# A channel fold by reflection, gate groups in half steps, and a last tile in column groups

## The chip, the cores and the metric

The program runs on all 8 cores of one Trainium2 chip. Each core holds one sequence of the batch (4096 positions, 1024 channels), and the cores exchange nothing. A time is the device time in microseconds (us) of the slowest core. Engines are named as in the profile: PE (TensorE matmul), PEld (its weight loads), DVE (VectorE), ACT (ScalarE), POOL (GpSimd), SP (SyncE, which here only issues transfers). L412 is line 412 of the kernel.

## The reference

Two layers with plain residual adds, then a final RMSNorm. `rms_norm` divides by the root mean square over 1024 channels.

```python
def fourier_mixer(h, w_in, w_out):            # layer 0
    proj = h @ w_in                           # (S, 2E), E = 2048
    xin, z = proj[..., :E], proj[..., E:]
    xg = xin.reshape(b, s, 8, 256)            # 8 groups of 256 channels
    y = fft2(xg, axes=(1, 3), norm="ortho").real
    return (y * silu(z)) @ w_out
def sgu_mixer(h, ...):                        # layer 1, chunks of 128 positions
    proj = h @ w_in                           # (S, 3E)
    u, v = gelu(proj[..., :2 * E]) split in two
    z = proj[..., 2 * E:]
    v = layer_norm(v) ; v = w_s[g] @ v (per chunk, per group) + b_s
    return (u * v * silu(z)) @ w_out
for i in range(2):
    x = x + mixer[i](rms_norm(x, norm[i]), ...)
return rms_norm(x, final_norm)
```

## The kernel before

Five instruction streams are recorded by hand in one program order. A small class `Q` per engine adds the semaphore waits that the buffers of an instruction ask for; each engine then runs its own instructions strictly in the order in which they were recorded. Six PSUM banks `pf0` to `pf5` are handed out in turn by `next_f()`, whatever the use, so the seventh user of a bank since the first waits until the first was read out. Two more banks, `pb`, serve the transposes.

Layer 0 runs in these stages.

- Stage A, 32 steps `s`, one tile of 128 positions each. SP loads the tile `xt`, ACT squares and sums it (`square`, L391), POOL adds eps and takes the power -0.5 (`norm`, L399 and L401), DVE scales to bf16 `xn` (L403), PE transposes it (L495), DVE writes it into `hT` times the norm weight `g0T` (L500). PE also multiplies the tile by `tr`, the first factor of the position transform (L475), ACT and DVE copy the result to `U` (L269, L271), and SP stores it to `Ud` in DRAM. In between PE works off gate groups from the list `zq`: `zgroup(hb, zt)`, L412, is 8 matmuls of 512 positions into one bank, closed by one SiLU on ACT (L416) into `sz`. The order of the six first loads and three small constants (`ident`, `tr`, `gT`) is written out ahead of the loop, all on SP. Up to step 23 the factor matmuls run one step late (the list `due`); from step 24 they run in their own step.
- Block transform, `qd` from 7 down to 0. SP reads `Ud` back in another layout as `V`. For each `qd` and each of 8 channel blocks `dc`, PE does 4 matmuls of 128 columns against the table `bdt` (L571) into one bank; ACT or DVE, whichever has the smaller planned load (`ev_engine`), scales it into `H` (L558, L560). A whole gate group stands behind `dc` 3. For `qd` 0 a small matmul per `dc` (L579) gives four further columns.
- Fold, once per channel group `g` (`fold`, L431). The channel DFT is folded into the input projection: 256 rows of the branch weight, cast to bf16 by a POOL transfer (`load_wb`, buffers `wb`), are multiplied by a 256x256 table `fmat` of cosines and sines, two matmuls of 256 columns for each `dc`. ACT copies the four banks to `wp`, then one column to `wsp` (L438) and zeros over it (L440).
- Per group: `pq(g)`, L608, multiplies `wp` with `H`; ACT and DVE split the result into `Dt` and `St`; DVE multiplies them onto the gates in `sz` (`gate`, L639), and SP stores to `gy`. Then `fold(g + 1)` and the gate groups of later `zt` (`zall`). `tick()` spreads the casts of later weights (`precasts`, POOL transfers `w0d` and `wind`) and the stores over these steps. `last_column()` (L676) uses `wsp` in group 6.

Layer 1 runs eight rounds of four tiles (L764, L839, L866, L876). Its last tile is `last_tile`: two halves of 512 columns are added (L776) and squared (L778), POOL forms the factor (L780, L782), DVE applies factor and norm weight in one instruction per half (L786), and SP and ACT store one half each. The program ends with a barrier on all queues.

## Time and profile before

| what | value |
|---|---|
| median of 3 runs (lowest, highest) | 1567.16 us (1565.13, 1567.92) |
| profiled execution, its own time | 1564.49 us |
| span of its slowest core | 1563.1 us (cores 1561.1 to 1563.1) |
| PE busy | 1533.1 us, 98% |
| DVE, ACT, POOL busy | 48%, 33%, 10% |
| granted TensorE clock, mean | 0.998 |
| share of PE in the chain that ended last | 97% |
| stage A ends, first block matmul | 115.54 us |
| `pq(0)` starts | 149.73 us |
| first layer-1 matmul (L839) | 447.26 us |
| last matmul of the program issued | 1553.72 us |

The span runs from the first to the last instruction on a core; the execution's own time is 1.4 us longer. Busy times of PE are of modelled ends of pipelined matmuls, so a stretch is better read from the start of one row to the start of the next: `8 matmuls of a gate group` start 1.73 us apart from the next group. A row that says `[1.77 <-DVE U_70 L271]` was idle for 1.77 us before it, and what ended that was the DVE instruction of line 271 that wrote `U`.

### The profile page before, as it was taken

To read this page: it belongs to the slowest core of one execution; us is meant where nothing else is said; L and a number is where in the kernel's file an instruction comes from. 1 tells how busy PE (TensorE), PEld (TensorE's weight loads), DVE (VectorE), ACT (ScalarE), POOL (GpSimd) and SP (SyncE) were. 2 spreads that over 40 slices of the span, in tenths; PEclk is the share of its full clock that TensorE was granted. 3 is DMA by queue.
4 is the path that set the end of the run, shared out by engine and by line. 5 is a ranking of instruction groups with operands and counts; after the bars stand their busy time and mean duration, and the time that the engine had idled before them with its cause. 6 is when DMAs were issued, how large, how long until landed. Compare 5 with 4: busy or idle time off the path is not lost.

```text
span 1563.1 us, 25441 instructions; the slowest of 8 cores (1561.1 to 1563.1 us)
## 1 busy us (share of the span) xinstructions
PE 1533.1 (98%) x8458; PEld 779.5 (50%) x8458; DVE 744.1 (48%) x1241; ACT 517.5 (33%) x919; POOL 156.7 (10%) x336
## 2 busy tenths in 40 slices
PE   6999999999999999999999999999999999999997
PEld 3546766546744444544444454444444444544443
DVE  5767532212657335624543463356346435624552
ACT  6756333333233213322331332133123313322331
POOL 3311111110211011001001100110010011001000
PEclk9999999999999999999999999999999999999999
DMA  9976999999879933632464165345325632643411
GB/s 247 299 246 176 174 137 148 152 145 149 253 249 263 255 110 103 205 142 78 162 193 137 28 219 175 106 138 193 135 55 189 203 101 73 199 167 88 147 49 55
DMA packets 103299, 247.74 MB, mean 158 GB/s; under 512 B 40042, under 2 KB 56042, under 8 KB 87402
## 3 DMA queue, kind: packets, MB, share of 16 engines
q1 hardware_dynamic: 53652, 207.76, 41.5%
q0 software_dynamic: 15568, 29.63, 15.0%
q10 hardware_dynamic: 33952, 8.72, 2.9%
q8 instruction: 72, 1.18, 0.3%
q14 instruction: 55, 0.45, 0.1%
HBM read 225.24 MB, written 58.87 MB: 182 GB/s over the span
## 4 chain that ended last, share of the span: by engine, by line
PE 97%; DMA 1%; DVE 1%; issue 0%; ACT 0%; SPq 0%; POOL 0%; ACTq 0%; DVEq 0%; POOLq 0%
PE pf L764 28%; PE pf L866 28%; PE pf L839 14%; PE pf L412 14%; PE pf L608 7%; PE pf L876 2%; PE pf L431 1%; DMA a0x_55<-xt 1%; PE pf L571 1%; PE pb L495 1%; PE pf L475 1%; DMA gTs<-gT 0%; DVE hT L500 0%; SPq L166 0%; PE pf L676 0%
## 5 line engine op out<-in xcount | busy, mean ns | idle before, releaser
L764 PE MATMUL pf<-W_2523,u 128*128 128x512 bf16 x1024 | 222.3, 379 | 0.0
L764 PE MATMUL pf<-W_2512,gyt 128*128 128x512 bf16 x992 | 216.6, 379 | 0.0
L764 PEld LDWEIGHTS pf<-W_2523,u 128*128 128x128 bf16 x1024 | 100.2, 98 | 120.8
L764 PEld LDWEIGHTS pf<-W_2512,gyt 128*128 128x128 bf16 x992 | 97.1, 98 | 116.8
L869 ACT ACTIVATE u<-pf 128x512 bf16<-128x512 f32 x128 | 76.4, 597 | 164.0 <-PE pf L866 154.8
L843 ACT ACTIVATE v<-pf 128x512 f32<-128x512 f32 x128 | 75.2, 597 | 119.5 <-PE pf L839 102.2
L866 PE MATMUL pf<-h1T,ring_2519 128*128 128x512 bf16 x416 | 95.3, 379 | 0.0
L866 PE MATMUL pf<-h1T,ring_2518 128*128 128x512 bf16 x416 | 95.0, 379 | 0.0
L866 PE MATMUL pf<-h1T,ring_2522 128*128 128x512 bf16 x416 | 94.8, 379 | 0.0
L866 PE MATMUL pf<-h1T,ring_2520 128*128 128x512 bf16 x416 | 94.8, 379 | 0.0
L866 PE MATMUL pf<-h1T,ring_2521 128*128 128x512 bf16 x384 | 88.3, 379 | 0.0
L618 DVE TENSOR_TENSOR Dt_93<-pc_97,pf 128x256 bf16<-128x256 f32 x28 | 11.8, 421 | 144.4 <-PE pf L608 144.4
L880 DVE SCALAR_TENSOR_TENSOR ytmp_2531<-pf,gTs,TT 128x512 f32<-128x512 f32 x64 | 48.1, 751 | 47.9 <-PE pf L876 47.9
L755 POOL TENSOR_SCALAR sm_2545<-sm_2545 128x1 f32<-128x1 f32 x24 | 5.3, 221 | 617.5 <-ACT sqj L800 573.9
L866 PEld LDWEIGHTS pf<-h1T,ring_2518 128*128 128x128 bf16 x416 | 39.7, 98 | 43.4
L866 PEld LDWEIGHTS pf<-h1T,ring_2522 128*128 128x128 bf16 x416 | 39.7, 98 | 43.2
L866 PEld LDWEIGHTS pf<-h1T,ring_2520 128*128 128x128 bf16 x416 | 39.6, 98 | 43.2
L866 PEld LDWEIGHTS pf<-h1T,ring_2519 128*128 128x128 bf16 x416 | 39.6, 98 | 42.7
L869 ACT ACTIVATE sg_2542<-pf 128x512 bf16<-128x512 f32 x64 | 38.2, 597 | 68.1 <-PE pf L866 53.3
L869 ACT ACTIVATE sg_2543<-pf 128x512 bf16<-128x512 f32 x64 | 38.2, 597 | 65.4 <-PE pf L866 64.8
L608 PE MATMUL pf<-H,wp_84 128*128 128x260 bf16 x512 | 57.6, 274 | 0.0
L608 PE MATMUL pf<-H,wp_85 128*128 128x260 bf16 x512 | 57.4, 274 | 0.0
(298 smaller groups left out, 2308.8 us busy)
## 6 DMA issues: line engine op xcount, KB each, us to landing
ring_2519<-wind SPq DMA_DIRECT2D x20, 1024.0 KB, 8.2
ring_2520<-wind SPq DMA_DIRECT2D x19, 1024.0 KB, 7.7
ring_2521<-wind SPq DMA_DIRECT2D x19, 1024.0 KB, 7.2
ring_2522<-wind SPq DMA_DIRECT2D x19, 1024.0 KB, 7.8
ring_2518<-wind SPq DMA_DIRECT2D x19, 1024.0 KB, 7.8
gyt<-gy SPq DMA_DIRECT2D x7, 2048.0 KB, 16.2
wind<-w_in1p POOLq DMA_DIRECT2D x24, 512.0 KB, 46.7
V<-ud SPq DMA_DIRECT2D x32, 256.0 KB, 8.0
```

The costliest lines, as they stand in the source:

```text
L412: pe.op(lambda e: e.matmul(bank[:], w[:, dc, :], hT[:, dc, hb * 512:(hb + 1) * 512], start=(dc == 0), stop=(dc == 7)), [wb_, hTb[hb], hTal ...
L431: pe.op(lambda e: e.matmul(bank[:, h * 256:(h + 1) * 256], wb[wb_slot(2 * g + kc)][0][:, dc * 128:(dc + 1) * 128], fmat[:, kc, :], start=( ...
L475: pe.op(lambda e: e.matmul(bank[:], tr[:], xn_[:, h * 512:(h + 1) * 512], start=True, stop=True), [trb, xnb], [bb], waw=False)
L495: pe.op(lambda e: e.transpose(out=bank[:, dc * 128:(dc + 1) * 128], in_=xn_[:, dc * 128:(dc + 1) * 128], identity=ident[:]), [xnb, identb] ...
L608: pe.op(lambda e: e.matmul(bank[:, 0:HQ], w_[:, dc, cs * 128:(cs + 1) * 128], H[:, qd, dc, cs, :], start=(dc == 0), stop=(dc == 7)), [wpb, ...
L764: pe.op(lambda e: e.matmul(bank[:], lhs(kc), rhs[:, kc, nh * 512:(nh + 1) * 512], start=(kc == 0), stop=(kc == 15)), lb(kc) + rb(kc), [bb] ...
L839: pe.op(lambda e: e.matmul(bank[:], h1T[:, dc, t * 128:(t + 1) * 128], r_[:, dc, :], start=(dc == 0), stop=(dc == 7)), [h1Tb[t], rb], [bb] ...
L843: act.op(lambda e: e.activation(out=vj, in_=bank[:], func=AF.Gelu_apprx_tanh), [bb], [vjb])
L866: pe.op(lambda e: e.matmul(bank[:], r_[:, dc, c0:c0 + 128], h1T[:, dc, :], start=(dc == 0), stop=(dc == 7)), h1Tb + [rb], [bb], waw=False, ...
L869: act.op(lambda e: e.activation(out=out_ap, in_=bank[:], func=func), [bb], wb_)
L876: pe.op(lambda e: e.matmul(bank[:, t * 128:(t + 1) * 128], vhat[t][0][:, ct * 128:(ct + 1) * 128], wsT[:, ct // 2, :], start=True, stop=True),
L880: dve.op(lambda e: e.scalar_tensor_tensor(out=y_[:].rearrange("c (t p) -> c t p", p=128), in0=bank[:].rearrange("c (t p) -> c t p", p=128) ...
```

## The change

Five things are done together. The diff below is cut to its core; of `last_tile` it shows the added lines alone.

1. The fold uses the symmetry of the DFT. Row `c` and row `256 - c` of the branch weight (the rows 0 and 128 as a pair of their own) are loaded as f32 in pieces `st` (128 rows x 2 x 256) by SP, and POOL writes their sum and difference as bf16 into `eo`. The table falls to 128 rows: 129 cosine columns for the sums (`fE`) and 192 columns for the differences (`fO`, 64 of them shared with the first). Of the sixteen 256-column matmuls of a group, eight have 129 columns and eight 192. Channels within a group are reordered (`_HARM`) to fit, on the host, for the weights too. The casts through POOL's transfers (`load_wb`) go. 8 groups have 4 pieces each, 64 POOL instructions in all: pieces 0 to 3 in stage A, 4 to 11 in the block transform, the rest by `tick()`. The casts of later weights start at tick 10 and then come every third tick instead of every fourth.
2. A gate group may be cut in two halves of 4 matmuls (`zhalves`). In the block transform the first half stands behind `dc` 3 and the second behind `dc` 7, with the bank taken at the first. The small matmuls of `qd` 0 go into one bank, ahead of it, and are read out by two DVE instructions.
3. `fold(1)` moves from behind `pq(0)` to the end of the block transform.
4. Stage A: the three small constants go to ACT's queue; the factor matmuls run one step late up to step 30; the norms run two tiles ahead up to step 14 and three from 15 on (before: three from 10 on).
5. The last tile has column groups of 512, 256 and 256, each with its own 16 matmuls; DVE applies the norm weight per group ahead of the factor, and the factor is then applied by ACT to one half and by DVE to the other.

```diff
+            def eo_of(g):
+                return eo[g if g < 3 else 4 - g % 2]
+            def load_piece(n):
+                t_, b_ = st[n % 2 if 4 <= n < 12 else 0]
+                sp.dma(t_[:], wb_in[n // 4, n % 4], d_st[n % 2 if 4 <= n < 12 else 0], writes=[b_], waw=True)
+            def sum_piece(n):
+                t_, b_ = st[n % 2 if 4 <= n < 12 else 0]
+                eo_, eob = eo_of(n // 4)
+                q = n % 4
+                for k, op in enumerate((ALU.add, ALU.subtract)):
+                    pool.op(lambda e: e.tensor_tensor(out=eo_[:, k, q * 256:(q + 1) * 256], in0=t_[:, 0, :],
+                                                      in1=t_[:, 1, :], op=op), [b_], [eob], waw=False)
+            folded = {"n": 0, "summed": 12}
+            def sums():
+                for n in range(12, 32):
+                    while n >= 20 and folded["n"] < n // 4 - 1:
+                        yield
+                    load_piece(n)
+                    for _ in range(4):
+                        yield
+                    sum_piece(n)
+                    folded["summed"] += 1
+                    yield
+                    yield
 
...
+                for _ in zhalves(hb, zt):
+                    pass
+            def zhalves(hb, zt):
 
                 w, wb_ = wz[zt % 6]
                 o, ob = sz[zt % 6]
                 bank, bb = next_f()
                 for dc in range(8):
+                    if dc == 4:
+                        yield
...
+                while folded["summed"] < 4 * g + 4:
+                    next(summing)
                 for d2 in dcs:
                     bank, bb = next_f()
                     for h in range(2):
                         dc = 2 * d2 + h
-                        for kc in range(2):
-                            pe.op(lambda e: e.matmul(bank[:, h * 256:(h + 1) * 256],
-                                                     wb[wb_slot(2 * g + kc)][0][:, dc * 128:(dc + 1) * 128], fmat[:, kc, :],
-                                                     start=(kc == 0), stop=(kc == 1)),
-                                  [wb[wb_slot(2 * g + kc)][1], cpkb], [bb], waw=False, inc=(h == 1 and kc == 1))
+                        for k, f, a, z in ((0, fE, 0, 129), (1, fO, 64, 256)):
+                            pe.op(lambda e: e.matmul(bank[:, h * 256 + a:h * 256 + z], eo_[:, k, dc * 128:(dc + 1) * 128], f,
+                                                     start=(k == 0), stop=True, skip_group_check=(k == 1)),
+                                  [eob, cpkb], [bb], waw=False, inc=(h == 1 and k == 1))
...
+            act.dma(ident[:], c_id[:, :], d_const, writes=[identb])
+            act.dma(gT[:], gT_in[:, :], d_cg, writes=[cG])
+            act.dma(tr[:], c_tr[:, :], d_tr[0], writes=[trb])
+            for t in range(NX):
+                load_x(t)
...
-            then = {0: [1], 1: [], 2: [], 3: [4], 4: [6], **{s: [s + 2] for s in range(5, 10)}, 10: [12, 13]}
+            then = {0: [1], 1: [], 2: [], 3: [4], 4: [6], **{s: [s + 2] for s in range(5, 15)}, 15: [17, 18]}
...
-                due.append(s)
-                while len(due) > (s < 24):
-                    transform(due.pop(0))
+                if s > 0:
+                    transform(s - 1)
                 for _ in range((s != 4) + (s % 4 == 3 and s < 16)):
                     if zq:
                         zgroup(*zq.pop(0))
+                if s == 31:
+                    transform(s)
...
-                if s in (12, 14):
-                    load_wb(s // 2 - 6)
+                if s in (12, 16, 20, 24):
+                    sum_piece(s // 4 - 3)
+                if s in (8, 12, 16, 20):
+                    load_piece(s // 4 - 2)
+                if s in (28, 29):
+                    load_piece(s - 24)
...
-                if ticks["n"] % 4 == 1:
+                if ticks["n"] > 8 and ticks["n"] % 3 == 1:
                     next(casts, None)
+                next(summing, None)
...
+                halves = zhalves(*zq.pop(0))
...
-                    if qd > 0 and dc == 3:
-                        zgroup(*zq.pop(0))
...
+                    if dc % 4 == 3:
+                        next(halves, None)
                 if 0 < qd < 5:
                     fold(0, [4 - qd])
+                for n in ((4,), (5, 6), (7,), (8,), (9,), (10,), (11,), ())[7 - qd]:
+                    sum_piece(n)
+                    if n < 10:
+                        load_piece(n + 2)
                 if qd == 0:
-                    load_wb(2)
-                    load_wb(3)
-                    for i in range(6, 9):
+                    fold(1, range(4))
+                    for i in (6, 7, 10):
                         load_wz(i)
-                    load_wb(4)
-                    load_wb(5)
-                    for i in range(9, 11):
-                        load_wz(i)
-                    for _ in range(2):
-                        next(casts, None)
-            zgroup(*zq.pop(0))
...
+            def last_tile(n):
 
                 x_, xb = x1[n % NX1]
+                y_, yb = x1[(n + 1) % NX1]
                 sm_, smb = sm[n % 4]
+                cols = [slice(0, 512), slice(512, 768), slice(768, 1024)]
+                xh = [Buf(f"xh{h}") for h in range(3)]
+                yh = [Buf(f"yh{h}") for h in range(3)]
+                for h, c in enumerate(cols):
+                    bank, bb = next_f()
+                    w = c.stop - c.start
+                    for kc in range(16):
+                        pe.op(lambda e: e.matmul(bank[:, 0:w], u[:, kc, 384:512], W1[:, kc, c],
+                                                 start=(kc == 0), stop=(kc == 15)),
+                              [ub[kc], W1b[kc // 4]], [bb], waw=False, inc=(kc == 15))
+                    dve.op(lambda e: e.tensor_tensor(out=x_[:, c], in0=x_[:, c], in1=bank[:, 0:w], op=ALU.add),
                            [bb, xb], [xh[h]])
                     act.op(lambda e: e.activation(out=sqj[:, c], in_=x_[:, c], func=AF.Square, scale=1.0 / 32.0,
                                                   accum_out=sm_[:, h:h + 1]), [xh[h]], [sqjb, smb], waw=False)
+                    if h == 1:
+                        pool.op(lambda e: e.tensor_scalar(out=sm_[:, 0:1], in0=sm_[:, 0:1], scalar1=EPS, scalar2=sm_[:, 1:2],
+                                                          op0=ALU.add, op1=ALU.add), [smb], [smb], waw=False)
+                    dve.op(lambda e: e.tensor_tensor(out=y_[:, c], in0=x_[:, c], in1=gFt[:, c], op=ALU.mult),
+                           [xh[h], gFb], [yb, yh[h]], waw=False)
+                pool.op(lambda e: e.tensor_tensor(out=sm_[:, 0:1], in0=sm_[:, 0:1], in1=sm_[:, 2:3], op=ALU.add), [smb], [smb])
                 pool.op(lambda e: e.tensor_tensor(out=sm_[:, 0:1], in0=sm_[:, 0:1], in1=mhalf[:], op=ALU.pow),
                         [smb, mhalfb], [smb])
+                for h, c in ((0, cols[0]), (1, slice(512, 1024))):
+                    if h == 0:
+                        act.op(lambda e: e.activation(out=y_[:, c], in_=y_[:, c], func=AF.Copy, scale=sm_[:, 0:1]),
+                               [yh[0], smb], [yh[0]])
+                    else:
+                        dve.op(lambda e: e.tensor_scalar(out=y_[:, c], in0=y_[:, c], scalar1=sm_[:, 0:1], scalar2=None,
+                                                         op0=ALU.mult), [yh[1], yh[2], smb], [yh[1]])
+                    (act, sp)[h].dma(out[n * 128:(n + 1) * 128, c], y_[:, c], d_last[h], reads=[yh[h]], writes=[outb])
```

How the instructions stand, at three places. First PE at the start of the block transform (`V` is its input, `wz` a gate group's weights, `pf` the bank written), before, the rest of `qd` 7 and the head of `qd` 6:

```order
L571 MATMUL pf3<-bdt_92,V_52 128x128 x4
L412 MATMUL pf4<-hT_51,wz3_81 128x512 x8
L571 MATMUL pf5<-bdt_92,V_52 128x128 x4
L571 MATMUL pf0<-bdt_92,V_52 128x128 x4
L571 MATMUL pf1<-bdt_92,V_52 128x128 x4
L571 MATMUL pf2<-bdt_92,V_52 128x128 x4
L571 MATMUL pf3<-bdt_92,V_52 128x128 x4
L571 MATMUL pf4<-bdt_92,V_52 128x128 x4
L571 MATMUL pf5<-bdt_92,V_52 128x128 x4
```

and after the change, the same place:

```order
L623 MATMUL pf3<-bdt_91,V_52 128x128 x4
L450 MATMUL pf4<-hT_51,wz3_81 128x512 x4
L623 MATMUL pf5<-bdt_91,V_52 128x128 x4
L623 MATMUL pf0<-bdt_91,V_52 128x128 x4
L623 MATMUL pf1<-bdt_91,V_52 128x128 x4
L623 MATMUL pf2<-bdt_91,V_52 128x128 x4
L450 MATMUL pf4<-hT_51,wz3_81 128x512 x4
L623 MATMUL pf3<-bdt_91,V_52 128x128 x4
L623 MATMUL pf4<-bdt_91,V_52 128x128 x4
```

The gate group in `pf4` stood whole between two blocks of the same `qd`; it now ends only behind the last block of its `qd`, and the second block of the next `qd` takes the same bank `pf4` again, one block after it.

Second POOL in stage A around step 12 (`stats` are the norm's sums, `wb` the cast weight, `eo` the sums of the fold), before:

```order
L399 TENSOR_SCALAR stats_47<-stats_47 128x1
L401 TENSOR_TENSOR stats_47<-stats_47,mhalf_49 128x1
L166 DMA wb0_86<-wbT 128x1024
L399 TENSOR_SCALAR stats_47<-stats_47 128x1
L401 TENSOR_TENSOR stats_47<-stats_47,mhalf_49 128x1
```

and after:

```order
L431 TENSOR_SCALAR stats_47<-stats_47 128x1
L433 TENSOR_TENSOR stats_47<-stats_47,mhalf_49 128x1
L397 TENSOR_TENSOR eo0_86<-st0_99 128x256 x2
L431 TENSOR_SCALAR stats_47<-stats_47 128x1
L433 TENSOR_TENSOR stats_47<-stats_47,mhalf_49 128x1
```

A transfer for the fold stood between the norms of two tiles; now two POOL computations stand there, and the next tile's norm behind them.

Third DVE at the end of the program (`x1` are the tiles, `gFt` the final norm weight, `sm` the factor), before:

```order
L894 SCALAR_TENSOR_TENSOR x1_4_2538<-x1_4_2538,sm1_2546,gFt_2537 128x1024
L894 SCALAR_TENSOR_TENSOR x1_0_2514<-x1_0_2514,sm2_2547,gFt_2537 128x1024
L776 TENSOR_TENSOR x1_1_2515<-x1_1_2515,pf4 128x512
L776 TENSOR_TENSOR x1_1_2515<-x1_1_2515,pf5 128x512
L786 SCALAR_TENSOR_TENSOR x1_1_2515<-x1_1_2515,sm3_2548,gFt_2537 128x512 x2
```

and after:

```order
L825 TENSOR_TENSOR x1_1_2569<-x1_1_2569,pf3 128x512
L832 TENSOR_TENSOR x1_2_2570<-x1_1_2569,gFt_2591 128x512
L825 TENSOR_TENSOR x1_1_2569<-x1_1_2569,pf4 128x256
L832 TENSOR_TENSOR x1_2_2570<-x1_1_2569,gFt_2591 128x256
L825 TENSOR_TENSOR x1_1_2569<-x1_1_2569,pf5 128x256
L832 TENSOR_TENSOR x1_2_2570<-x1_1_2569,gFt_2591 128x256
L842 TENSOR_SCALAR x1_2_2570<-x1_2_2570,sm3_2602 128x512
```

The norm weight stands in instructions of its own behind each add, and behind the factor only one instruction of 512 columns is left on DVE.

## Rows read from the trace of the kernel before

**Rows 1.** The page's engine part: busy us, share of the span, instructions.

```profile
PE 1533.1 (98%) x8458; PEld 779.5 (50%) x8458; DVE 744.1 (48%) x1241; ACT 517.5 (33%) x919; POOL 156.7 (10%) x336
```

**Rows 2.** The chain that ended last: start us, us, what; two stretches of folds.

```profile
270.58 1.75 PE pf L431 x16
...
385.33 3.51 PE pf L431 x32
```

**Rows 3.** Timeline of PE, block transform: start us, us, instruction, count, idle before.

```profile
115.54 1.06 PE L571 MATMUL pf<-bdt,V 128*128 128x128 bf16 x16
116.43 1.89 PE L412 MATMUL pf<-hT,wz_81 128*128 128x512 bf16 x8
118.16 1.78 PE L571 MATMUL pf<-bdt,V 128*128 128x128 bf16 x28
...
120.23 0.38 PE L571 MATMUL pf<-bdt,V 128*128 128x128 bf16 x4 [0.29 <-ACT H L558]
...
149.73 14.35 PE L608 MATMUL pf<-H,wp_84 128*128 128x260 bf16 x128
```

**Rows 4.** Timeline of ACT there: a gate group's SiLU, then read-outs of blocks.

```profile
118.42 0.60 ACT L416 ACTIVATE sz_75<-pf 128x512 bf16<-128x512 f32 x1 [0.86 <-PE pf L412]
...
119.40 2.42 ACT L558 ACTIVATE H<-pf,g0s 128x512 bf16<-128x512 f32 x4 [0.38 <-PE pf L571]
```

**Rows 5.** Waits of PE: who waited for whom, us in total, times, longest.

```profile
PE pf L676 <- ACT wsp L438: 0.3, 1, 0.3
```

**Rows 6.** Timeline of all engines at the start, first tiles of stage A.

```profile
8.48 1.01 PE L495 MATMUL pb<-ident,a0xn_60 128*128 128x128 bf16 x8 [8.48 <-DVE a0xn_60 L403]
...
10.65 1.23 DVE L500 TENSOR_TENSOR hT<-pb,gTs 128x1024 bf16<-128x1024 bf16 x1 [2.44 <-DMA gTs<-gT]
...
11.79 0.76 DVE L403 TENSOR_SCALAR a0xn_61<-a0x_55,stats 128x1024 bf16<-128x1024 f32 x1
12.15 0.83 POOL L401 TENSOR_TENSOR stats<-stats,mhalf 128x1 f32<-128x1 f32 x1
12.64 0.33 SPq L166 DMA_DIRECT2D a0x_55<-xt  x1
```

**Rows 7.** Busy us by engine, clock, DMA share and GB/s, in two stretches.

```profile
10.00:20.00 10.00, 5.99 (x37) 3.40 (x38) 7.46 (x8) 7.19 (x14) 6.66 (x12) 1.00 1.03 253
...
150.00:200.00 50.00, 50.00 (x374) 36.23 (x372) 25.42 (x80) 17.85 (x39) 12.40 (x21) 1.00 1.04 170
```

**Rows 8.** Timeline of PE at step 24 of stage A.

```profile
83.40 1.89 PE L412 MATMUL pf<-hT,wz_81 128*128 128x512 bf16 x8 [1.77 <-DVE U_70 L271]
```

**Rows 9.** Timeline of POOL in stage A, one norm and the next.

```profile
77.38 0.57 POOL L401 TENSOR_TENSOR stats<-stats,mhalf 128x1 f32<-128x1 f32 x1 [0.21 <-POOL stats L399]
79.60 0.22 POOL L399 TENSOR_SCALAR stats<-stats 128x1 f32<-128x1 f32 x1 [1.65 <-ACT a0xn_61 L391]
```

**Rows 10.** POOL by shape: count, busy us and mean ns, idle before.

```profile
L639 POOL TENSOR_TENSOR szsp<-p_100,szsp 8x1792 bf16<-8x1792 f32 x1 | 3.3, 3289 | 0.1
...
L639 POOL TENSOR_TENSOR szsp<-p_100,szsp 8x224 bf16<-8x224 f32 x1 | 0.6, 610 | 0.1
```

**Rows 11.** Timeline of all engines over the last tile.

```profile
1539.74 13.98 PE L764 MATMUL pf<-W_2523,u 128*128 128x512 bf16 x64
...
1547.88 1.06 ACT L800 ACTIVATE sqj<-x_0_2514 128x1024 bf16<-128x1024 f32 x1 [5.76 <-DVE x_0_2514 L797]
...
1553.83 0.69 DVE L776 TENSOR_TENSOR x_1_2515<-x_1_2515,pf 128x512 f32<-128x512 f32 x1 [1.36 <-PE pf L764]
1554.61 0.63 ACT L778 ACTIVATE sqj<-x_1_2515 128x512 bf16<-128x512 f32 x1 [1.33 <-DVE x_1_2515 L776]
...
1556.75 1.42 DVE L786 SCALAR_TENSOR_TENSOR x_1_2515<-x_1_2515,sm_2548,gFt 128x512 f32<-128x512 f32 x2 [2.24 <-POOL sm_2548 L782]
...
1558.25 0.38 ACTq L166 DMA_DIRECT2D out<-x_1_2515  x1
```

**Rows 12.** Timeline of DVE: an add of 256 columns from PSUM.

```profile
151.84 0.42 DVE L618 TENSOR_TENSOR Dt_93<-pc_97,pf 128x256 bf16<-128x256 f32 x1 [3.19 <-PE pf L608]
```

More of the change, by code:

```diff
@@ L19 @@
 HQ = 260
+_HARM = [*range(0, 128, 2), *range(1, 128, 2)]
 def _chan_order():
@@ L23, in _chan_order @@
     for g in range(8):
-        o += [g * 256 + m for m in range(128)]
-        o += [g * 256 + 128] + [g * 256 + 256 - m for m in range(1, 128)]
+        o += [g * 256 + m for m in _HARM]
+        o += [g * 256 + 128] + [g * 256 + 256 - m for m in _HARM[1:]]
     return np.array(o)
@@ L65, in rows @@
         return a.reshape(4, 32, -1).transpose(1, 0, 2).reshape(128, -1)
-    pk = np.concatenate([Fm.reshape(128, 512), rows(B64)], axis=1)
+    pk = np.concatenate([FE, np.zeros((128, 1)), FO, rows(B64)], axis=1)
     bdt = np.stack([rows(BD[pr]) for pr in range(32)], axis=1)
@@ L347, in build @@
             wp = [tile(f"wp{i}", [128, 8, 256], BF16) for i in range(2)]
-            wb = [tile(f"wb{i}", [128, D], BF16, (top["at"] - 4096 if i < 2 else vh + 2048 * (i - 2)) + 2048 * (i % 2 if i < 2 else 0))
-                  for i in range(6)]
+            eo = [tile(f"eo{i}", [128, 2, D], BF16, o) for i, o in enumerate((top["at"] - 4096, wzo, wzo + 4096, vh + 4096, vh))]
             bdt, bdtb = tile("bdt", [128, 32, 128], BF16, top["at"])
@@ L354, in build @@
             wsT, wsTb = tile("wsT", [128, 8, 128], BF16)
+            st = [tile("st0", [128, 2, 256], F32, top["at"] - 2048), tile("st1", [128, 2, 256], F32, top["at"] - 4160)]
             assert top["at"] <= nc.sbuf_usable_end, (top["at"], nc.sbuf_usable_end)
@@ L363, in build @@
             d_wz = [dsem(f"d_wz{i}") for i in range(6)]
-            d_wb = [dsem(f"d_wb{i}") for i in range(6)]
+            d_st = [dsem(f"d_st{i}") for i in range(2)]
             d_gy = [dsem(f"d_gy{i}") for i in range(6)]
@@ L515, in build @@
                     sp.dma(Ud[r, 0:128, :], U[r % 8][0][:], d_us[r % 8], reads=[U[r % 8][1]], writes=[Udb])
-                for n in then.get(s, [s + 3] if 10 < s < 29 else []):
+                for n in then.get(s, [s + 3] if 15 < s < 29 else []):
                     norm(n)
@@ L564, in build @@
             for qd in range(7, -1, -1):
+                halves = zhalves(*zq.pop(0))
+                if qd == 0:
+                    bank, bb = next_f()
+                    for dc in range(8):
+                        pe.op(lambda e: e.matmul(bank[:, dc * 64:(dc + 1) * 64], V[:, 0, dc * 128:(dc + 1) * 128], b64,
+                                                 start=(dc == 0), stop=(dc == 7)), [Vb[0], cpkb], [bb], waw=False, inc=(dc == 7))
+                    for c in range(2):
+                        dve.op(lambda e: e.tensor_tensor(
+                            out=H[:, :, :, c, 256:260].rearrange("d q e t -> d e q t"),
+                            in0=bank[:].rearrange("d (e c q t) -> d c e q t", c=2, q=8, t=4)[:, c],
+                            in1=g0s[:].rearrange("d (e q t) -> d e q t", q=1, t=1).broadcast_to([128, 8, 8, 4]),
+                            op=ALU.mult), [bb, g0sb], Hb, waw=False, cost=cd(256))
                 for dc in range(8):
@@ L903, in build @@
                 if g == 0:
-                    fold(1, range(4))
                     for hb in range(6, 8):
@@ L919, in build @@
                     fold(g + 1, range(4))
+                if g == 1:
+                    for i in (8, 9):
+                        load_wz(i)
                 for zt in zafter[g]:
```

78 lines of the change are left out of this document (25 added, 53 removed).

## The prediction

> **What bounds the kernel now.** I read the engine part of the page first, then the chain that ended last, then the waits of PE, and last the timelines of the stretches that the change touches. PE is busy for 98% of the span [rows 1], so only two things can move the time: columns that PE no longer streams, and stretches in which PE stands still. From the first `pq` at 149.73 us to its last matmul at 1553.7 us PE runs without a gap worth naming, and a matmul taken out there is worth its full length. The gaps lie in three places: stage A, the block transform, and the tail behind the last matmul. The change has an edit in each, beside the shorter fold.
>
> **The fold, groups 2 to 5.** A group is sixteen matmuls of 256 columns in 1.75 us [rows 2], 109.4 ns each. Sixteen of 128 columns take 116.43 - 115.54 = 0.89 us [rows 3], 55.6 ns each, so a column costs (109.4 - 55.6) / 128 = 0.42 ns. 129 columns are 56.0 ns and 192 are 82.5 ns; eight such pairs are 1.11 us in place of 1.75 us, 0.64 us less. Four groups stand between PE work that never waits: **-2.57 us**, between -2.3 and -2.7.
>
> **Groups 6 and 7** follow each other (3.51 us, [rows 2]) and would give 1.29 us. But PE already waits 0.3 us for the `wsp` of group 7 [rows 5], behind eight read-outs on ACT that do not get shorter. These begin when the first bank is full, after 0.28 us in place of 0.44 us. I take that 0.16 us, **-0.16 us**; the ends are 0 and -1.29 us.
>
> **The block transform, with groups 0 and 1.** Today the stretch takes 149.73 - 115.54 = 34.19 us [rows 3], and group 1 another 1.75 us behind `pq(0)`: 35.94 us. PE's own work in the new stretch, per `qd`: eight blocks of 0.222 us and one gate group of 118.16 - 116.43 = 1.73 us [rows 3] are 3.51 us. The half steps even out the read-outs, since a half group of 0.86 us now stands behind every four blocks. But the bank does not follow. It is taken at the first half, is full only after the second, and five banks are handed out in between or right behind. The order rows show it: `pf4` is ended by the second half, then comes one block in `pf3`, and the next block wants `pf4` again. It must wait for the SiLU. From the end of a gate group to the SiLU's start are 118.42 - 118.16 = 0.26 us [rows 3, 4], the SiLU takes 0.60 us [rows 4], and from the end of a read-out on ACT (119.40 + 2.42 / 4 = 120.01) to PE's next matmul at 120.23 are 0.22 us [rows 3, 4]: 1.08 us. One block covers 0.22 us of it, so PE stands for 0.86 us; where a part of the fold (0.28 us) stands there, 0.80 us. That gives 4.37 us for each of three `qd` without fold, 13.1 us; 3.51 + 0.28 + 0.80 = 4.59 us for each of four with it, 18.4 us; for `qd` 0 3.51 us and at most 0.44 us for its small matmuls; then group 1, 1.11 us, with the same wait of 0.80 us inside it. Sum 37.4 us, **+1.4 us**. If the wait were not there it would be 37.4 - 3 x 0.86 - 5 x 0.80 = 30.8 us, -5.1 us; if ACT were each time at the start of another read-out of 0.60 us, +6.2 us. I stay at the worked value, since in the 0.86 us of the second half ACT can finish what the four blocks left it.
>
> **Stage A.** Three terms. First, at step 24 two tiles' factor matmuls fall together and PE waits 1.77 us for a bank [rows 8]. With the steps late by one throughout, this goes; at step 31 a gate group now stands between the two: -1.8 us. Second, `hT` of the first tile waits 2.44 us for `gT`, which SP issued behind three tiles; DVE starts it at 10.65 us though PE's transposes ended at 8.48 + 1.01 = 9.5 us, so DVE, the next norm and with it the next load at 12.64 us are about 1.0 us late [rows 6]. On ACT's queue `gT` leaves ahead of the tiles. But the transfer engines are full in that stretch, share 1.03 [rows 7], so an earlier issue is only partly an earlier landing: I take half, -0.5 us, between 0 and -1.0. Third, POOL gets two sums of 256 elements for each of four pieces, between the norms of two tiles. The nearest rows are sums over 8 partitions: 3289 ns for 1792 elements, 610 ns for 224 [rows 10], 1.71 ns an element and 0.66 us for 256. Two with the gaps between them are 1.5 us, and POOL idles 1.65 us a step [rows 9]. They fit, just; for the piece that lands late I add 0.3 us. Upper end: 128 partitions could cost more than 8; at 2.0 us a sum the pair exceeds the idle by 2.5 us, four times: 10 us. Stage A: **-2.0 us**, between -2.8 and +8.
>
> One mechanism speaks against this. POOL's power instruction took 0.83 us at 12.15 us [rows 6] where it takes 0.57 us elsewhere [rows 9], and it ran while DVE's norm at 11.79 us occupied its 0.76 us: POOL was held up by 0.26 us. The Trainium skill, page "SBUF — State Buffer", section "Who interferes with whom", says that DVE and GpSimd share one pair of ports as an exclusive lock, so that a DVE instruction in a two-port mode or with two SBUF inputs and a GpSimd instruction block each other for a whole instruction. By that rule the trace agrees, and what it would do is the second rival below.
>
> **The tail.** PE ends at 1539.74 + 13.98 = 1553.72 us, and the last store is issued 4.53 us later, at 1558.25 us [rows 11]. The last add falls from 0.69 us to 0.42 us for 256 columns [rows 11, 12]. The square falls by (1.06 - 0.63) / 2 = 0.215 us [rows 11]. POOL keeps two instructions. In place of 1.42 us for two DVE instructions in a row one of 512 runs beside one on ACT, some 0.6 us (0.63 us for an ACT row of 512 with a sum). That is 0.27 + 0.215 + 0.8 = 1.3 us; the multiplications that now stand between the adds on DVE may cost 0.1 us: **-1.2 us**, between -0.5 and -1.6. PE's columns stay 1024.
>
> **At no cost.** The pieces from 12 on, the paced casts and the moved weight loads run while PE never waits, in a stretch where the transfer engines are full anyway (share 1.04, [rows 7]); each fold has its four pieces summed at least 9 ticks, 16 us, ahead. If that cover went, PE would wait for a landing at a fold.
>
> **Sum.** -2.57 - 0.16 + 1.4 - 2.0 - 1.2 = -4.5 us. The rows come from an execution of 1564.49 us (span 1563.1 us), which would become 1560.0 us. That execution lies 2.7 us under the median of the runs shown; taken off the median, 1567.16 us, the forecast is 1562.6 us.
>
> **Rivals.** *The half steps do as they look:* the bank wait is hidden and the block transform becomes PE's own work. For it: today's waits there are only 0.3 us each [rows 3]. Against it: the bank order above. -11.0 us, 1556.2 us.
>
> *No change that can be told:* stage A gives nothing. Tiles land no earlier in a full transfer stretch, and a norm on DVE in the way of a pair of sums, as in rows 6, lengthens the pair by 0.76 us to 2.3 us, 0.6 us over POOL's idle, four times, 2.4 us. For it: [rows 6, 7]. Against it: the 1.77 us of step 24 has nothing to do with either. Stage A then stands near 0, and the sum is -2.5 us, 1564.7 us.
>
> *Slower:* the sums on POOL hold up the norms, and PE waits for transposes at steps 12 to 24. SP waits with POOL, since the next piece needs the buffer `st0`, and the next tiles' loads stand behind it in SP's queue. Against it: the 0.66 us of rows 10, if partitions work side by side. It decides from about 1.75 us a sum (3.7 us a pair, 2.0 us over the idle, 8 us in all, which turns -4.8 us into +3.1 us); at 2.0 us a sum it is +5.4 us, 1572.6 us.
>
> **How the numbers follow.** Forecast 0.52, half steps as they look 0.10, no change 0.26, slower 0.12. A measurement of this kernel tells about 0.2% from no change, 3.1 us. The forecast's own range is 1559.5 to 1565.0 us, of which 0.85 lies beyond 3.1 us. Faster: 0.44 + 0.10 + a fifth of the no-change case, 0.05, about 0.6. Same: 0.08 + 0.19 + 0.03, 0.3. Slower: 0.1, nearly all from the slow case. The range, 1558.0 to 1567.5 us, leaves out most of the first rival and of the slow one.
>
> **What would show it.** Right: folds of 1.11 us where 1.75 us stood; PE waits of about 0.8 us on `sz` in each `qd` of the block transform, and about 37 us from the first block matmul to `pq(0)`; no wait at step 24; 3.2 us from the last matmul to the last store's issue. Wrong: no waits on `sz` there (first rival), first block matmul not earlier than 115 us (second), sums of over 1.5 us and PE waiting for norms after step 12 (third), or PE waiting on `eo` or on `sz` stores behind 150 us, for which I see no cause.

## The result and the profile after

The change made the kernel slower: 1585.22 us (median of 4 runs, 1583.14 to 1587.31) beside 1567.16 us of the kernel before on the same chip, a ratio of 1.0118 [1.0096, 1.0140] (in brackets the 95% interval), some 18 us. Medians and ratios, here and below, are of undisturbed executions; some others ran longer, at a lower granted clock on one die or both, and are left out. The forecast was 1562.6 us and faster. The cores of the traced execution, which lay within 2 us before, now spread from 1571.2 to 1585.0 us. All rows of after are of core 1, the slowest. The waits of PE between 150 and 420 us (who waited for whom, us in total, times, longest), where before there was only the `wsp` of [rows 5]:

```profile
PE pf L450 <- ACT sz_74 L454: 16.7, 1, 16.7
PE pf L472 <- POOL eo_89 L397: 4.9, 1, 4.9
PE pf L650 <- ACT wp_84 L480: 1.0, 1, 1.0
```

The first two are the two that the last paragraph of the prediction named as having no cause in sight. The chain that ended last, traced in this stretch (start us, us, what), shows what stands behind them:

```profile
183.03 1.14 PE pf L472 x16
185.93 1.79 POOL eo_89 L397 x2
187.79 10.54 DMA st_99<-wbE
...
331.40 0.72 POOL eo_90 L397
332.19 11.01 DMA st_99<-wbE
344.04 0.72 POOL eo_90 L397
344.83 11.33 DMA st_99<-wbE
356.34 0.65 issue
356.99 0.72 POOL eo_90 L397
358.31 15.57 DMA gy<-sz_74
373.96 0.61 ACT sz_74 L454
374.70 19.45 PE pf L450 x80
```

From 186 to 358 us the path is no longer PE but a ladder, and each of its rungs has two parts: a piece lands (10 to 17 us), POOL sums it, and only then can SP ask for the next one, since there is one tile `st0`. The same on SP's queue (start us, us from the first to the last of the run of issues, count):

```profile
199.95 43.72 SPq L172 DMA_DIRECT2D st_99<-wbE  x4
243.81 0.47 SPq L172 DMA_DIRECT2D gy<-sz_76  x1
244.43 0.57 SPq L172 DMA_DIRECT2D gy<-sz_77  x1
256.64 44.16 SPq L172 DMA_DIRECT2D st_99<-wbE  x4
...
316.61 41.50 SPq L172 DMA_DIRECT2D st_99<-wbE  x4
358.31 0.47 SPq L172 DMA_DIRECT2D gy<-sz_74  x1
```

A row of four issues is the time from the first to the fourth, so three rungs: they take 41 to 44 us, and a pair of stores stands between each four. (The expectations below call such a row "four pieces".) On POOL the casts stand behind the sums, so a late piece holds them back too, and each rung then lets out two casts at once (timeline of POOL, `wind` is a cast; "idle before" shows the wait for the piece):

```profile
241.86 1.40 POOL L397 TENSOR_TENSOR eo_90<-st_99 128x256 bf16<-128x256 f32 x2 [10.27 <-DMA st_99<-wbE]
243.22 1.39 POOL L172 DMA_DIRECT2D wind<-w_in1p  x2
255.15 1.42 POOL L397 TENSOR_TENSOR eo_90<-st_99 128x256 bf16<-128x256 f32 x2 [10.54 <-DMA st_99<-wbE]
```

The store of `sz_74` leaves at 358.31 us, lands at 374, and until then the SiLU that refills `sz_74` may not run: PE fills six banks and stands. After its stand it does not even start at full speed. The windows (length, busy us of PE, PEld, DVE, ACT and POOL with counts, granted clock, DMA share, GB/s):

```profile
349.00:358.00 9.00, 8.99 (x42) 3.88 (x40) 0.00 (x0) 0.00 (x0) 1.70 (x3) 1.00 1.01 115
358.00:374.70 16.70, 0.00 (x0) 0.03 (x1) 0.00 (x0) 0.74 (x2) 3.79 (x6) 0.61 0.99 200
374.70:380.20 5.50, 5.50 (x17) 2.04 (x18) 0.00 (x0) 2.90 (x6) 0.00 (x0) 0.62 0.99 166
380.20:394.00 13.80, 13.80 (x66) 6.24 (x65) 0.00 (x0) 4.78 (x8) 3.48 (x5) 1.00 0.71 122
```

In the 16.7 us without a matmul the granted clock was 0.61 in the mean; it was 1.00 at their start and 0.50 at their end, the lower of the two levels (1.2 of 2.4 GHz). The next 17 matmuls took 5.5 us where 42 took 9.0 us before the stand: about 1.9 us more. The 4.9 us for `eo` were lost earlier: the fold of group 5 starts at 316.78 us, at a granted clock of 0.52 from 316 to 321 us, and takes 2.10 us in place of 1.14. So 4.9 + 1.0 + 16.7 + 1.9 = 24.5 us are lost between 311 and 380 us on this core. The wait for `sz_74` is there on all eight cores (7.8 to 19.7 us), that for `eo` on two.

The other parts lost nothing of this. Block transform, timeline of PE:

```profile
114.31 1.05 PE L623 MATMUL pf<-bdt,V 128*128 128x128 bf16 x16
...
117.82 0.39 PE L623 MATMUL pf<-bdt,V 128*128 128x128 bf16 x4
118.82 0.83 PE L623 MATMUL pf<-bdt,V 128*128 128x128 bf16 x12 [0.61 <-ACT sz_75 L454]
...
151.00 1.16 PE L650 MATMUL pf<-H,wp_84 128*128 128x260 bf16 x9
```

It takes 36.7 us with group 1, against 35.94, the same on every core. It begins at 114.31 us; [rows 3] with 115.54 are of core 7, and on core 1 it began at 114.31 before, too. The bank wait on the SiLU is there in each `qd`, about 0.6 us long. The tail, timeline of all engines:

```profile
1569.50 7.11 PE L822 MATMUL pf<-W_2577,u 128*128 128x512 bf16 x48
...
1579.91 0.38 ACTq L172 DMA_DIRECT2D out<-x_2_2570  x1
```

1579.91 - 1576.61 = 3.30 us from the last matmul to the last store's issue, 4.53 us before [rows 11].

### The profile page after: what moved, and what is told of

It reads as the page before. It is cut to its first block, busy times and chain, and to the rows that moved or that the text cites. A ratio compares the mean times of both kernels' runs of the same rounds, so it can differ in the third digit from the quotient of the medians.

```text
span 1585.0 us, 25600 instructions; the slowest of 8 cores (1571.2 to 1585.0 us)
## 1 busy us (share of the span) xinstructions
PE 1535.2 (97%) x8474; PEld 780.1 (49%) x8474; DVE 749.6 (47%) x1241; ACT 519.4 (33%) x919; POOL 196.6 (12%) x385
## 4 chain that ended last, share of the span: by engine, by line
PE 83%; DMA 11%; issue 2%; POOL 1%; ACT 1%; DVE 1%; SPq 0%; POOLq 0%; DVEq 0%; ACTq 0%
PE pf L921 28%; PE pf L806 27%; PE pf L894 14%; DMA st_99<-wbE 9%; PE pf L450 5%; PE pf L650 4%; PE pf L931 2%; DMA gy<-sz_74 1%; PE pf L623 1%; PE pb L529 1%; PE pf L509 1%; DMA a0x_56<-xt 1%; DVE hT L534 1%; POOL eo_90 L397 0%; POOL eo_89 L397 0%
## 5 line engine op out<-in xcount | busy, mean ns | idle before, releaser
L806 PE MATMUL pf<-W_2577,u 128*128 128x512 bf16 x992 | 215.4, 379 | 0.0
L806 PEld LDWEIGHTS pf<-W_2577,u 128*128 128x128 bf16 x992 | 97.1, 98 | 117.0
L806 PEld LDWEIGHTS pf<-W_2566,gyt 128*128 128x128 bf16 x992 | 97.1, 98 | 116.8
L450 PE MATMUL pf<-hT,wz_80 128*128 128x512 bf16 x192 | 45.3, 391 | 16.7 <-ACT sz_74 L454 16.7
L921 PEld LDWEIGHTS pf<-h1T,ring_2573 128*128 128x128 bf16 x416 | 39.6, 98 | 42.7
L650 PE MATMUL pf<-H,wp_84 128*128 128x260 bf16 x512 | 57.6, 274 | 1.0 <-ACT wp_84 L480 1.0
```

The costliest lines, as they stand in the source:

```text
L450: pe.op(lambda e: e.matmul(bank[:], w[:, dc, :], hT[:, dc, hb * 512:(hb + 1) * 512], start=(dc == 0), stop=(dc == 7)), [wb_, hTb[hb], hTal ...
L650: pe.op(lambda e: e.matmul(bank[:, 0:HQ], w_[:, dc, cs * 128:(cs + 1) * 128], H[:, qd, dc, cs, :], start=(dc == 0), stop=(dc == 7)), [wpb, ...
L806: pe.op(lambda e: e.matmul(bank[:], lhs(kc), rhs[:, kc, nh * 512:(nh + 1) * 512], start=(kc == 0), stop=(kc == 15)), lb(kc) + rb(kc), [bb] ...
L921: pe.op(lambda e: e.matmul(bank[:], r_[:, dc, c0:c0 + 128], h1T[:, dc, :], start=(dc == 0), stop=(dc == 7)), h1Tb + [rb], [bb], waw=False, ...
```

## The experiments

At first two readings of the ladder were open: that it is itself the bound (S), or that only SP's order is, which lets the stores wait (O). The first four runs were to tell these apart and to price the rest of the change.

**Stores off SP.** Edit:

```
- stores.append(lambda: sp.dma(
+ stores.append(lambda: (act if kc < 12 else sp).dma(
```

> The changed kernel with the gate products' stores (gy) issued by ACT in place of SP; the piece loads stay on SP through their one staging tile. Theory S (the 20 pieces of groups 3 to 7 go one after the other through one tile, about 12 us each, from 157 to 397 us, and that chain alone is the bound): the wait of 16.7 us for sz_74 goes, the pieces still end near 395 us, PE waits some 20 us for eo at the folds of groups 6 and 7 instead, and the time stays at 1580 to 1588 us. Theory O (only the order on SP costs: stores stand behind loads that wait for their tile): 1585.2 - 16.7 = 1568.5 us, and the wait for eo stays at 4.9 us or less.

1581.53 us, ratio 1.0096 [1.0066, 1.0125]. On core 1, SP's queue and the waits of PE:

```profile
154.67 239.59 SPq L172 DMA_DIRECT2D st<-wbE  x19
```

```profile
PE pf L472 <- ACT wp L275: 8.5, 1, 8.5
PE pf L472 <- POOL eo L397: 4.5, 1, 4.5
```

The wait for `sz` is gone, the ladder still runs on (the last piece is asked for at 394 us), and PE stands at the folds instead (17.7 us on core 2, the slowest). S holds: moving the stores moves the wait and gives little back, and the place of the stores on SP is not by itself the cause.

**Two half tiles.** Pieces 12 to 31 in halves of 128 columns that alternate in `st0`:

```
+ sh = [tile(f"sh{i}", [128, 2, 128], F32, top["at"] - 2048 + 1024 * i) for i in range(2)]
...
+ sum_half(m)
+ load_half(m + 2)
```

> The changed kernel with pieces 12 to 31 cut into halves of 128 columns that alternate between two 1 KB tiles in the place of the one 2 KB tile, so that two loads are under way. Theory S (each load is long because it stands in line in full transfer engines, 10.7 us whatever else is asked of them, and one at a time makes a chain): two at a time bring a half each 4 to 5 us, the 40 halves end by 360 us, no wait of PE over 1 us between 151 and 400 us, 1585.2 - 21.6 = 1563.6 us (1561 to 1567). Rival B (the share of the engines sets it: two loads under way take twice as long each): still 12 us for 256 KB, 1580 to 1588 us.

1590.34 us (two executions), ratio 1.0137 [1.0099, 1.0175]; PE waits 14.7 us for `sz` and 8.1 us for `eo` on core 1. A half lands in 12.7 us (median from 200 to 350 us), as long as a whole piece, two of them under way. 256 KB still cost some 12 us, as rival B had it. My figure for S was wrong here, since two halves are no more bytes under way than one piece. A half is also 256 rows of 512 B where a whole piece is 128 rows of 2 KB, so this run does not tell time in line from the cost of small rows. The casts themselves landed in 12.2 us here, so the halves were not slow because of a longer line of casts.

**Casts behind the last sum.** Edit, in `tick`:

```
- if ticks["n"] > 8 and ticks["n"] % 3 == 1:
-     next(casts, None)
```

> The changed kernel with no cast among the ticks: all 32 casts of later weights are issued by POOL behind the last sum. Theory S: without the casts in the engines a piece lands in 4 to 6 us in place of 10.7, the chain of pieces is no longer late, PE waits nowhere over 1 us from 151 to 375 us; what the late casts cost afterwards is open (they need some 225 us of full engines and are read from about 400 us on), so 1560 to 1575 us. Rival O (the order on SP, not the landing): the wait for sz_74 stays at 8 to 17 us, and pieces land as slowly where a store is ahead of them.

1679.16 us, ratio 1.0702 [1.0681, 1.0723], far from the expected 1560 to 1575 us, but the place is another. POOL issues the late casts in its own order, with at most eight under way (the program has eight semaphores for them), and stands at them until 496 us. Its own gate products come behind them; DVE waits 101.3 us for them, and PE 97.1 us for DVE (core 5). The stretch in question is clean. SP's queue, and the transfers from 150 to 330 us (KB each, median us to landing):

```profile
275.27 15.73 SPq L172 DMA_DIRECT2D st<-wbE  x4
...
318.21 15.63 SPq L172 DMA_DIRECT2D st<-wbE  x4
```

```profile
gy<-sz SPq DMA_DIRECT2D x10, 1024.0 KB, 5.3
st<-wbE SPq DMA_DIRECT2D x18, 256.0 KB, 4.0
```

In the changed kernel the same loads, from 200 to 350 us, show 11.4 us (the row stands with the run at the old pace below). So the long landing is the casts' doing, and without them three rungs take 15.7 us in place of 41 to 44 us.

**The change without the fold.** The kernel before with the edits of stage A, block transform and last tile, and nothing of the fold, its loads and the pace of the casts.

> The kernel before with the other parts of the change alone: constants on ACT's queue and the transform one step late in stage A, half gate groups and the joint 64-column product in the block transform, the last tile in three column groups; fold, its loads and the casts as before. If the trace of the changed kernel is read rightly, stage A gives 1.2, the block transform costs 0.8 to 1.4 and the tail gives 1.2: 1566 us (1564 to 1568), no wait between 150 and 400 us. If one of these parts is what made the change slow: 1575 us or more.

1563.68 us (1562.61 to 1564.39), ratio 0.9966 [0.9951, 0.9981], just under the range expected, and no wait behind 150 us but that of [rows 5]. These parts are no cause of the loss. Its block transform takes 149.74 - 114.41 = 35.3 us with the old fold matmuls, 34.19 before: the half steps (with the joint small product) cost 1.1 us.

The second four asked which condition the ladder needs: the pace of the casts, the single tile, or the way of the weights.

**Casts at the old pace.** Edit:

```
- if ticks["n"] > 8 and ticks["n"] % 3 == 1:
+ if ticks["n"] % 4 == 1:
...
+ for _ in range(2):
+     next(casts, None)
```

> The changed kernel with the casts at the pace of before (two ahead, then one at every fourth tick from the first). Theory S (a load's time in line behind the casts, one load at a time): the casts fill the engines from 151 us on in place of 170, the 20 pieces still take 240 us or more, PE waits 15 to 30 us in all between 150 and 420 us, 1580 to 1592 us. Rival P (the denser pace, one at every third tick, is what fills the engines and makes the loads long): pieces land in 7 us or less, 1564 to 1570 us.

1560.24 us, ratio 0.9977 [0.9968, 0.9987]: faster than before, with the pieces, the single tile and SP's order all as in the changed kernel. My theory said that the pace makes no difference, and it fell here; the rival's 7 us for a piece did not come either. Three rungs on SP (core 1) take 30 us:

```profile
248.04 30.29 SPq L172 DMA_DIRECT2D st<-wbE  x4
...
289.76 31.05 SPq L172 DMA_DIRECT2D st<-wbE  x4
```

The stretch from 200 to 350 us in the changed kernel, and then in this one (the window; the busy tenths of the transfer engines in 40 slices; landing of pieces and of casts):

```profile
200.00:350.00 150.00, 145.08 (x883) 85.94 (x882) 40.34 (x120) 50.06 (x98) 33.97 (x46) 0.98 1.03 141
DMA  9999999999999999999999999999999999999999
st_99<-wbE SPq DMA_DIRECT2D x11, 256.0 KB, 11.4
wind<-w_in1p POOLq DMA_DIRECT2D x19, 512.0 KB, 24.5
```

```profile
200.00:350.00 150.00, 150.00 (x916) 88.00 (x914) 40.17 (x120) 52.57 (x103) 36.92 (x50) 1.00 0.99 159
DMA  9999999999999999999599999999394999999968
st<-wbE SPq DMA_DIRECT2D x13, 256.0 KB, 9.5
wind<-w_in1p POOLq DMA_DIRECT2D x20, 512.0 KB, 14.6
```

A share of 0.99 in place of 1.03 looks like nothing, but here the engines now and then run dry, and in the changed kernel they never do. A cast of that stretch lands in 14.6 us here and in 24.5 us in the changed kernel: there, a line has formed. Counted in time the casts of the changed kernel are hardly denser (22 in that stretch, 3 of them of `w0d`, against 20). The difference is what goes with a piece: two casts to each rung there, one and two in turn here. The 20 sums here start 11.2 us apart in the mean, which is their six ticks, so the ladder keeps time.

**Casts later and denser.** `if ticks["n"] > 40 and ticks["n"] % 2 == 1`.

> The changed kernel with the casts from tick 41 on, one at every second tick (they end at tick 103 in place of 106, so the bytes before 400 us are the same). Theory S: the pieces up to the fold of group 3 (8 of them) land in 4 to 5 us; the other 12 take some 12 us each from 230 us on, to 375 us; PE waits 0 to 8 us, 1563 to 1572 us. Rival P: as late as with the pace of the changed kernel, 1580 us or more.

1585.13 us, ratio 1.0136 [1.0118, 1.0154], with 20.3 us of waiting for `eo` on core 1. The time is the rival's and not mine. While no or few casts run, three rungs take 30.8 us (in which SP also waits for gates), behind that 39.1, 45.2 and 48.6 us. The 375 us that I worked out for the last sum came out at 402. Not all of this is landing: in two of the later rungs (sums at 343.0 and 367.1 us) POOL did not wait for the piece but stood at casts that had to wait for earlier casts.

**Three tiles at the new pace.** Two more tiles of 2 KB in the slots of gate weights 10 and 11, which are loaded later; pieces 12 to 20 and 27 to 31 use all three:

```
+ s3 = [st[0]] + [tile(f"s3{i}", [128, 2, 256], F32, wzo + 2048 * (4 + i)) for i in range(2)]
```

> The changed kernel with three staging tiles of 2 KB for pieces 12 to 20 and 27 to 31 (two of them in the places of gate weights 10 and 11, which are loaded after piece 20 in place of 151 us), one tile for 21 to 26 as in the changed kernel. Casts and stores as there. Theory S (every load stands in line some 10 us whatever its size, so more of them under way bring more bytes; the two half tiles brought none because each held half as much): pieces 12 to 20 and 27 to 31 at 4 to 6 us each, the last sum by 350 us, no wait of PE over 2 us between 151 and 400 us, 1563.6 us (1561 to 1568). Rival B (the share of the engines sets the bytes that come, however many loads are under way): 12 us for each piece, PE waits as before, 1580 us or more.

1560.40 us, ratio 0.9963 [0.9926, 1.0000]. The engines are as full (share 1.05, with 25 casts from 200 to 350 us) and a piece lands as late (10.8 and 16.8 us), but up to three are under way for 14 of the 20 pieces, and PE waits only the 1.0 and 0.3 us of folds 6 and 7. The pieces also stand earlier on SP, ahead of the stores, so the run frees the order on SP along with the tile.

**Rows loaded by the casting queue, summed in place.**

```
- load_piece(n)
- sum_piece(n)
+ pool.dma(eo_of(g)[0][:], wr_in[g], d_wr[g % 2], ...)
+ for q in range(4): ...  # b = a - b; a = a + a; a = a - b on 256 columns
```

> The changed kernel with the weights of groups 3 to 7 loaded as in the kernel before, by POOL's casting queue (one load of 512 KB written for each group, straight into the fold's tile in bf16, groups 3 and 4 at the end of the block transform, group g + 2 after fold g), and summed in place there (three operations on 256 columns, four times a group). No staging tile, no piece load on SP. Theory S: without the chain of pieces there is nothing late; the stores go as in the kernel before, PE waits under 2 us between 151 and 400 us, and the folds keep their gain: 1563.7 us of the parts without fold, less 2.6 for folds 2 to 5, 0.2 for 6 and 7 and some 1.0 for 0 and 1: 1560 us (1558 to 1564). Rival Q (a load behind the casts on POOL's own queue is as late as a piece): PE waits 5 us or more for eo, 1567 us or more.

1559.68 us, ratio 0.9972 [0.9961, 0.9983], at the new pace and a share of 1.03. One load of a group stands in the full line as well (34.8 us, and POOL waits 15.5 to 17.5 us for each of the last three), but it is asked for 54 to 109 us ahead of its fold (core 1), and PE does not wait for it.

The old pace had undone two edits at once, the start and the density. The next two part them.

**Late start, every fourth tick.** `if ticks["n"] > 8 and ticks["n"] % 4 == 1`.

> The changed kernel with its late start of the casts (none up to tick 8, none ahead) but the pace of before, one at every fourth tick: of the two edits that the run at the old pace undid together, the pace alone is undone. Theory D (the pace decides: a cast each 7.6 us leaves the engines room for a piece in 7 to 9 us, a cast each 5.7 us does not, and the chain of pieces takes 11 us each): four pieces on SP in 38 us or less, no wait of PE over 1 us between 151 and 400 us, 1560 to 1564 us. Rival T (the start decides: the casts that the first 12 ticks no longer take are met by the pieces later): waits of 10 us or more, 1575 us or more.

1574.77 us (three executions), ratio 1.0066 [1.0044, 1.0088]. Three rungs take 27 to 36 us, and from 151 to 400 us PE has only the 1.0 and 0.3 us of folds 6 and 7 to wait, so D is right on the ladder. But the time is not 1560 us: four casts are left over and are issued in a bunch at 370 us, the stores behind that land late, and the load of `gyt` for layer 1 is issued at 406.7 us in place of 390.3 at the old pace. That the bunch is what slows the stores is argued, not tried. Core 5, waits of PE (5.1 to 7.2 us on cores 4 to 6):

```profile
PE pf L806 <- DMA gyt<-gy: 7.2, 1, 7.2
```

**Early start, every third tick.** `if ticks["n"] % 3 == 1`, and two casts ahead.

> The other half of it: casts from the first tick and two ahead, as before, but one at every third tick. Theory D: four pieces on SP take 41 us or more while casts run, PE waits 8 to 25 us in all, 1572 to 1590 us. Rival T: the early start alone is enough, 1560 to 1564 us.

1580.99 us, ratio 1.0097 [1.0077, 1.0117]; three rungs take 39 to 41 us up to 344 us, PE waits 10.9 us for `sz` on core 1 and 15.2 us for `sz` and 4.5 us for `eo` on core 0. D holds, T falls.

**Two versions with whole gate groups** in the block transform, to take back the 1.1 us.

> A version meant to beat both: rows of groups 3 to 7 loaded by POOL's casting queue and summed in place (as in the run of that name), and the gate groups of the block transform whole again, after the fourth of eight products as in the kernel before. Read from the traces the half steps cost 1.1 us there (35.3 us against 34.2 with the same folds): 1559.7 - 1.1 = 1558.6 us (1557.5 to 1560). Rival: the bank waits of 0.6 us come back at other places and the time is that of half steps, 1559.7 us.

> The changed kernel with the casts at the pace and start of before and whole gate groups in the block transform: 1560.4 - 1.1 = 1559.3 us (1558 to 1561). Rival as with the rows in place: 1560.4 us; and one more, that the moved SiLUs and stores bring the pieces behind again, 1565 us or more.

1558.03 us, ratio 0.9964 [0.9950, 0.9978], and 1559.10 us, ratio 0.9962 [0.9948, 0.9977]. The first is the lowest median of all; the two can't be told apart by their intervals, nor from the run without the fold (0.9966 [0.9951, 0.9981]), so what the fold itself gives stands in its rows and not in these times. The first one's block transform with the folds of groups 0 and 1 runs from 112.99 to 147.29 us, 34.3 us, where the changed kernel takes 36.7 us. With the short folds whole groups are thus 2.4 us quicker there, on every core and in both versions, and not 1.1 us (PE, core 0):

```profile
112.99 1.05 PE L631 MATMUL pf<-bdt,V 128*128 128x128 bf16 x16
113.88 1.89 PE L457 MATMUL pf<-hT,wz 128*128 128x512 bf16 x8
...
147.29 2.93 PE L661 MATMUL pf<-H,wp 128*128 128x260 bf16 x25
```

## Why the prediction was wrong, and where it was right

**The step that failed** is the paragraph "At no cost", in its sentence that "each fold has its four pieces summed at least 9 ticks, 16 us, ahead". That counted where the sums stand in the program. It took for granted that a piece is there when its sum's turn comes. A piece with its sum has six ticks, about 11 us; it needs 11.4 us to land in the median, up to 17.3, and 1.4 us for the sum (POOL, two operations of 256 columns). From the fourth sum at 198.47 us to the fifteenth at 356.30 a rung takes 14.3 us in the mean, 3 us more than it has. Beside the run at the old pace (core 1 of both) the sums come 3 us later at the sixth, 16 us at the ninth and 26 us at the twelfth, for which the fold of group 5 waits. The trace of before could have shown it: that "the transfer engines are full anyway" was my reason for calling a transfer free, where it is a reason for pricing it by its landing in that stretch. The gy stores of before, from 150 to 400 us on core 1 (KB each, median us to landing), showed that line:

```profile
gy<-sz_72 SPq DMA_DIRECT2D x2, 1024.0 KB, 14.0
gy<-sz_73 SPq DMA_DIRECT2D x2, 1024.0 KB, 18.5
```

Without casts such a store takes 5.3 us. The list also leaves out SP's own order: the longer of the two waits, 16.7 us, is for a store that stands behind late pieces.

The second half of the same error: I put "the paced casts" in the list of things at no cost. Without the pieces they are (rows in place, 1559.68 us at the new pace), and the pieces are with the casts at the old pace (1560.24 us). Together they cost 0.0141 of the time, the ratio of 1.0118 less that of 0.9977, some 22 us. The loss needs both of two conditions: one piece under way at a time (it goes with three tiles, and with one load per group), and casts at every third tick or closer (at every fourth tick the ladder keeps time, at every third it falls behind, and an early or a late start changes neither). That PE has to pay for it takes too little slack at the folds or at the stores behind the pieces; that is read from the waits, and taking the stores off SP alone did not end it.

Why a load that stands alone is slow behind casts, the runs show only from outside: halves of 128 KB and pieces of 256 KB land alike (12.7 and 11.4 us), three pieces under way bring more than one. The cause of the long landing inside the engines stays open. The Trainium skill, page "DMA: Bandwidth & Descriptors", section "Queues, rings and completion order", says that each transfer engine takes turns between the queues that have work, packet by packet. By that rule a piece shares each engine with a cast for as long as casts are in line, and is quick when they run out. The trace agrees in that much: 11.4 us with a line, 9.5 us where it sometimes ran dry, 4.0 us without casts. No run here shows the packets themselves.

**The other steps**, by the forecast's terms:

| term | forecast, us | measured, us |
|---|---|---|
| folds 2 to 5 | -2.57 | 4 x (1.14 - 1.75) = -2.4 |
| folds 6 and 7 | -0.16 | 411.59 - 408.18 = 3.41, against 387.49 - 383.92 = 3.57: -0.16 |
| block transform, folds 0 and 1 | +1.4 | 36.69 - 35.94 = +0.75 |
| stage A | -2.0 | 114.40 - 114.44 = 0.0 (medians of the eight cores) |
| tail | -1.2 | 3.30 - 4.53 = -1.2 |
| sum | -4.5 | -3.0 |

The fold's matmuls and the tail were priced well from rows of other shapes. In folds 6 and 7 ACT indeed sets the end: the matmuls became shorter and the wait for `wp`, 1.0 us, took their place. The bank wait in the block transform came as drawn from the order, 0.6 us where 0.8 to 0.86 were worked out, so the first rival falls and the term came at half its size.

Stage A is not settled. In this pair of executions it ends no earlier (from 112.2 to 115.5 us by core, from 113.5 to 115.5 before), which is what the second rival said; in ten later ones, of versions with the same edits of stage A, the median of the cores lies between 112.1 and 113.5 us, 0.9 to 2.3 us earlier than in the one trace of before. Step 24 no longer waits, but later steps do, by up to 0.7 us each on `hT`, 1.3 us in all. The four pairs of sums on POOL took 1.86 us each there, where 1.5 us were forecast and POOL idled 1.65 us; DVE's norm ran beside each and took 1.07 us in place of 0.75. Behind 150 us a pair takes 1.41 us in the median. The slower rival needed 1.75 us for each sum; the kernel became slower, but not by that path.

Once the ladder is gone the kernel gains about that: at the old pace the ratio is 0.9977 [0.9968, 0.9987], -3.6 us (-5.0 to -2.0) of 1564.08. The -4.5 us of the forecast lie within it, but partly by luck, since the block transform cost less and stage A gave less in the pair of traces than was worked out, and the two misses cancel in part. The forecast was right in kind about the folds, the bank wait and the tail, and wrong about the stretch that it did not price.

## What to carry to other kernels

A transfer in a stretch where the transfer engines are full is not free: price it by its landing there. If it goes through one buffer, that landing plus the use of the buffer is the period of the whole series, and slack counted in program order pays for it only once. Before a queue gets transfers that wait for each other, list what stands behind them on that queue and who needs it; and see whether the engine that waits for the buffer also issues the transfers that compete with it, as POOL does here.

## What was not expected of the hardware

The share of the DMA engines tells little near 1: at 0.99 a piece took 9.5 us and a cast 14.6 us, at 1.03 a piece 11.4 us and a cast 24.5 us, and PE went from 1.3 us to 21.6 us of waits for banks and sums. With three tiles the share was 1.05 and a cast took 42.7 us, and PE did not wait for them at all.

Cutting a load in half did not make it land sooner: 128 KB in rows of 512 B, two loads under way, took 12.7 us, 256 KB in rows of 2 KB, one under way, 11.4 us.
